# Two of the four weight sums of each seven-product pair: from VectorE additions to a plain transfer and an adding one

## The reference, cut to what matters

```python
hn = rmsnorm(h, norm_mlp_g[l])
x = h + jnp.square(jax.nn.relu(hn @ w_up[l])) @ w_down[l]        # 1024 -> 4096 -> 1024
...
h2 = rms_norm(x, ln2_g[l])
x = x + (jax.nn.silu(h2 @ w_ffn_gate[l]) * (h2 @ w_ffn_up[l])) @ w_ffn_down[l]   # 1024 -> 2816 -> 1024
```

## Time and profile before

| | |
|---|---|
| median of three runs | 1889.53 us |
| the profiled execution, its own time | 1890.52 us |
| span of its trace (first to last instruction) | 1888.7 us |
| TensorE busy | 1878.7 us (99%), granted clock 0.999 |
| VectorE busy | 1244.8 us (66%) |
| ScalarE busy | 775.0 us (41%) |
| GpSimd busy | 1088.0 us (58%) |
| DMA | 176.78 MB, 94 GB/s in the mean |

### The profile page before, as it was taken

The page is one execution under the profiler, slowest core; times in us unless marked ns, Lnnn a source line. Parts: engine busy times, 40 slices in busy tenths (PEclk is TensorE's granted clock), DMA queues, the critical chain, the costliest instruction groups (busy, mean ns, idle before and its releaser), DMA issues.

```text
span 1888.7 us, 31897 instructions
## 1 busy us (share of the span) xinstructions
PE 1878.7 (99%) x11737; PEld 1604.7 (85%) x11737; DVE 1244.8 (66%) x2116; ACT 775.0 (41%) x1523; POOL 1088.0 (58%) x1223
## 2 busy tenths in 40 slices
PE   9999999999999999999999999999999999999998
PEld 7788888888888888899989888888888888999997
DVE  7876777767642247767775468787721367888882
ACT  5344433444342245333433544655432344333333
POOL 5454345443445477767776844444555585666665
PEclk9999999999999999999999999999999999999999
DMA  4312220222223332332334322122233223323232
GB/s 160 98 48 89 78 77 28 83 89 67 68 81 109 133 97 93 101 101 92 110 101 128 135 100 79 56 67 79 79 134 104 96 90 100 112 91 112 93 109 78
DMA packets 53470, 176.78 MB, mean 94 GB/s; under 512 B 7744, under 2 KB 8576, under 8 KB 53120
## 3 DMA queue, kind: packets, MB, share of 16 engines
q1 hardware_dynamic: 52880, 172.85, 27.9%
q10 hardware_dynamic: 496, 2.65, 0.4%
HBM read 171.26 MB, written 4.23 MB: 93 GB/s over the span
## 4 chain that ended last, share of the span: by engine, by line
PE 98%; DVE 1%; POOL 0%; DMA 0%; ACT 0%; issue 0%; DVEq 0%
PE bank L322 18%; PE bank L324 17%; PE bank L323 17%; PE bank L860 5%; PE bank L862 5%; PE bank L861 5%; PE bank L910 5%; PE bank L911 5%; PE bank L912 5%; PE bank L2066 2%; PE bank L2060 2%; PE bank L2077 1%; PE bank L2317 1%; PE bank L2304 1%; PE bank L1277 1%; PE bank L1294 1%
## 5 line engine op out<-in xcount | busy, mean ns | idle before, releaser
L311 POOL TENSOR_TENSOR slab_lo<-slab_raw,slab_hi 128x256 fp32r<-128x256 f32 x1140 | 994.8, 907 | 750.0 <-ACT slab_hi L304 749.9
L322 PE MATMUL bank<-u_hi,slab_hi 128*128 128x512 f32 x1048 | 443.4, 423 | 0.2
L324 PE MATMUL bank<-u_hi,slab_lo 128*128 128x512 f32 x1048 | 410.9, 392 | 0.0
L323 PE MATMUL bank<-u_lo,slab_hi 128*128 128x512 f32 x1048 | 409.2, 390 | 0.0
L304 ACT CAST slab_hi<-slab_raw 128x1024 fp32r<-128x1024 f32 (+1 forms) x302 | 298.7, 999 | 88.5 <-PE bank L324 49.2
L324 PEld LDWEIGHTS bank<-u_hi,slab_lo 128*128 128x128 f32 x1048 | 196.7, 188 | 43.3
L322 PEld LDWEIGHTS bank<-u_hi,slab_hi 128*128 128x128 f32 x1048 | 197.3, 188 | 39.7 <-issue 4.1
L323 PEld LDWEIGHTS bank<-u_lo,slab_hi 128*128 128x128 f32 x1048 | 197.8, 189 | 34.2 <-issue 1.9
L910 PE MATMUL bank<-part_hi,slab_hi 128*128 128x512 f32 x384 | 150.0, 391 | 0.6 <-DVE residual L1824 0.6
L911 PE MATMUL bank<-part_lo,slab_hi 128*128 128x512 f32 x384 | 149.7, 390 | 0.0
L912 PE MATMUL bank<-part_hi,slab_lo 128*128 128x512 f32 x384 | 149.5, 389 | 0.0
(11 more groups left out here) (444 smaller groups left out, 3990.2 us busy)
## 6 DMA issues: line engine op xcount, KB each, us to landing
slab_raw<-slabs SPq DMA_DIRECT2D x302, 512.0 KB, 3.5
g_and_cum_rows<-row_store SPq DMA_DIRECT2D x7, 512.0 KB, 6.4
residual<-x_t SPq DMA_DIRECT2D x4, 512.0 KB, 7.0
residual<-x_t SPq DMA_DIRECT2D x1, 2048.0 KB, 9.3
residual_store<-residual SPq DMA_DIRECT2D x1, 2048.0 KB, 8.9
residual<-residual_store ACTq DMA_DIRECT2D x1, 2048.0 KB, 9.5
out_t<-result_tok SPq DMA_DIRECT2D x4, 256.0 KB, 2.4
out_t<-residual SPq DMA_DIRECT2D x4, 256.0 KB, 2.6
```

Of the source, the lines that this page charges most:

```text
L311: ins = pool.tensor_tensor(w_lo[s][:, ks, :], raw[s][:, ks, :], w_hi[s][:, ks, :].bitcast(F32), ALU.subtract)
L322: pe.matmul(bank, w_hi[s][:, k, :], x_hi[:, k, :], start=first, stop=False)
L323: pe.matmul(bank, w_hi[s][:, k, :], x_lo[:, k, :], start=False, stop=False)
L324: mm = pe.matmul(bank, w_lo[s][:, k, :], x_hi[:, k, :], start=False, stop=last)
```

## The change

For every seven-product pair, u1 and u3 are no longer added by VectorE. SP issues two plain transfers of 256 KB each from the weights in HBM into `w_sums_raw` (b.k1 into u1, a.k1 into u3); GpSimd waits for their landing and issues two accumulating transfers (b.k2 onto u1, b.k1 onto u3), which count up a semaphore `u_added`. VectorE waits for `u_added` and makes u2 and u4 as before. SP waits, before its two transfers, for both low halves of the pair before (`fast_u_lo`), and issues them ahead of the load of the slab that follows the pair. GpSimd issues its two ahead of the splits of the down slabs for the next gate (or of the pair in front, in the first block), and ahead of the splits of the up slabs for an up pair. Two semaphores are reused under new names.

```diff
@@ load_slab @@
+            if j % 2 == 0 and (ph, j // 2 - 1) in fast_of:
+                w_sums_begin(sp, ph, j - 2, fast_of[ph, j // 2 - 1])
             wait_slab(sp, s_lo, ph, i, j)
             if (ph, j // 2 - 2) in fast_of:
-                wait_again(sp, "fast_sum", 4 * fast_of[ph, j // 2 - 2] + 4)
+                wait_again(sp, "fast_sum", 2 * fast_of[ph, j // 2 - 2] + 2)
@@ the sums @@
-        def w_sums_first(dve, ph, j, f):
-            sa, sb = ph.slot(j), ph.slot(j + 1)
-            if f > 0:
-                wait_again(dve, "fast_u_lo", 2 * f)
-            dve.wait_ge(s_raw[sb], ph.landed(0, j + 1))
-            dve.tensor_tensor(ws_raw[:, f_u1], raw[sb][:, k1, :], raw[sb][:, k2, :], ALU.add)\
-                .then_inc(again("fast_sum"), 1)
-            dve.wait_ge(s_raw[sa], ph.landed(0, j))
-            dve.tensor_tensor(ws_raw[:, f_u3], raw[sa][:, k1, :], raw[sb][:, k1, :], ALU.add)\
-                .then_inc(again("fast_sum"), 1)
+        def w_sums_begin(sp, ph, j, f):
+            if f > 0:
+                wait_again(sp, "fast_u_lo", 2 * f)
+            wait_again(sp, "x_sum", 4 * QT * (1 if ph is ph_mlp else 2))
+            sp.dma_start(w_form(f_u1), w_part(ph, j + 1, k1)).then_inc(again("u_begun"), 16)
+            sp.dma_start(w_form(f_u3), w_part(ph, j, k1)).then_inc(again("u_begun"), 16)
+
+        def w_sums_first(pool, ph, j, f):
+            wait_again(pool, "u_begun", 32 * f + 32)
+            pool.dma_start(w_form(f_u1), w_part(ph, j + 1, k2), accum_op=ALU.add).then_inc(sem("u_added"), 16)
+            pool.dma_start(w_form(f_u3), w_part(ph, j + 1, k1), accum_op=ALU.add).then_inc(sem("u_added"), 16)
+
+        def w_sums_ahead(pool, ph, j):
+            g = j // 2
+            if j % 2 == 0 and (ph, g) in fast_of and ph is ph_ffn and FFN_GROUPS[g][0] == "up":
+                w_sums_first(pool, ph, j, fast_of[ph, g])
+            if j % 2 == 0 and (ph, g + 1) in fast_of and not (ph is ph_ffn and FFN_GROUPS[g + 1][0] == "up"):
+                w_sums_first(pool, ph, j + 2, fast_of[ph, g + 1])
 
         def w_sums_second(dve, ph, j, f):
             sa = ph.slot(j)
-            wait_again(dve, "fast_sum", 4 * f + 1)
+            dve.wait_ge(sem("u_added"), 32 * f + 32)
+            dve.wait_ge(s_raw[sa], ph.landed(0, j))
             dve.tensor_tensor(ws_raw[:, f_u2], ws_raw[:, f_u1], raw[sa][:, k1, :], ALU.add)\
                 .then_inc(again("fast_sum"), 1)
@@ mlp_pool, and the same in ffn_pool @@
+                w_sums_ahead(pool, ph_mlp, j + LEAD)
                 split_lo(pool, ph_mlp, 0, j + LEAD, fast_slab_start(ph_mlp, j + LEAD))
@@ mlp_dve; in ffn_dve three such calls @@
-                    if after:
-                        w_sums_first(dve, ph_mlp, 2 * MLP_FAST[f + 1], f + 1)
```

More of the change, by code:

```diff
@@ L250, in program @@
                  "fast_u_hi": "edif", "fast_u_lo": "v_rhs", "x_raw": "osum", "x_sum": "k_rhs", "x_hi": "eg",
-                 "x_lo": "cols", "down_half": "qk_ps"}
+                 "x_lo": "cols", "down_half": "qk_ps", "u_begun": "blk_ps", "tok_ps": "rsc"}
         LATER = {old: new for new, old in AGAIN.items()}
@@ L538, in turn @@
                     mm = pe.transpose(tok_banks[t][:, c * P:(c + 1) * P], h_res[:, m, t * P:(t + 1) * P], ident[:])
-                mm.then_inc(sem("tok_ps"), 1)
+                mm.then_inc(again("tok_ps"), 1)
         def norm_pe(pe, n):
@@ L761, in out_dve @@
             norm_dve(dve, n)
-            if n == 1:
-                w_sums_first(dve, ph_mlp, 2 * MLP_FAST[0], 0)
             if n in X_NORMS:
@@ L814, in x_sums_lo, with w_part @@
                 .then_inc(again("x_lo"), 1)
-        def w_sums_first(dve, ph, j, f):
-            sa, sb = ph.slot(j), ph.slot(j + 1)
-            if f > 0:
-                wait_again(dve, "fast_u_lo", 2 * f)
-            dve.wait_ge(s_raw[sb], ph.landed(0, j + 1))
-            dve.tensor_tensor(ws_raw[:, f_u1], raw[sb][:, k1, :], raw[sb][:, k2, :], ALU.add)\
-                .then_inc(again("fast_sum"), 1)
-            dve.wait_ge(s_raw[sa], ph.landed(0, j))
-            dve.tensor_tensor(ws_raw[:, f_u3], raw[sa][:, k1, :], raw[sb][:, k1, :], ALU.add)\
-                .then_inc(again("fast_sum"), 1)
+        def w_part(ph, j, ks):
+            src = dram["slabs"][bass.ds(ph.index(0, j), 1), :, ks.start * P:ks.stop * P]
+            return src.rearrange("a p n -> (a p) n")
@@ new lines, in w_form @@
+        def w_form(u):
+            return ws_raw[:, u].rearrange("p k c -> p (k c)")
+        def w_sums_begin(sp, ph, j, f):
+            if f > 0:
+                wait_again(sp, "fast_u_lo", 2 * f)
[6 more added lines that the diff above has]
+            pool.dma_start(w_form(f_u3), w_part(ph, j + 1, k1), accum_op=ALU.add).then_inc(sem("u_added"), 16)
@@ L831, in w_sums_second @@
             dve.tensor_tensor(ws_raw[:, f_u2], ws_raw[:, f_u1], raw[sa][:, k1, :], ALU.add)\
                 .then_inc(again("fast_sum"), 1)
-            wait_again(dve, "fast_sum", 4 * f + 3)
+            wait_again(dve, "fast_sum", 2 * f + 1)
             dve.tensor_tensor(ws_raw[:, f_u4], ws_raw[:, f_u2], raw[sa][:, k2, :], ALU.add)\
@@ L837, in w_sums_hi @@
         def w_sums_hi(act, f, h):
-            wait_again(act, "fast_sum", 4 * f + 3 + h)
+            wait_again(act, "fast_sum", 2 * f + 1 + h)
             if f > 0:
@@ L1787, in ffn_act @@
             for t in range(NT):
-                act.wait_ge(sem("tok_ps"), t + 1)
+                wait_again(act, "tok_ps", t + 1)
                 act.activation(tok_out[:, t, :], tok_banks[t][:], ACT.Copy, scale=r_col[:, t:t + 1])\
@@ L1843, in ffn_dve @@
                             silu(q, 1)
-                    elif before:
-                        w_sums_first(dve, ph_ffn, j + 2, before)
                     wait_again(dve, "fast_prod", 5 * f + 2)
@@ L1864, in ffn_dve @@
                     elif before:
-                        w_sums_first(dve, ph_ffn, j + 4, before)
                         w_sums_second(dve, ph_ffn, j + 4, before)
@@ L1885, in ffn_dve @@
                         f = fast_of[ph_ffn, g + 1]
-                        w_sums_first(dve, ph_ffn, j + 2, f)
                         w_sums_second(dve, ph_ffn, j + 2, f)
@@ L1939, in ffn_pool @@
                 if j + LEAD < ph_ffn.n:
+                    w_sums_ahead(pool, ph_ffn, j + LEAD)
                     split_lo(pool, ph_ffn, 0, j + LEAD, fast_slab_start(ph_ffn, j + LEAD))
```

## The result

The changed kernel takes 2010.2 us (median of 4 runs, 2007.7 to 2013.9) where the kernel before takes 1889.9 beside it: ratio 1.0637, 95% interval 1.0624 to 1.065. The profiled execution took 2009.6 us with a span of 2007.8. The forecast was 1938. So the direction was right, and 120 us stand where 48 were forecast: inside the range of 1898 to 2025, but in its part over 1975, which had a chance of 0.25.

The account below looks back on a forecast made before the run. TensorE, busy 1878.7 of 1888.7 us, was taken to bound the kernel. Late sums cost 46.5 us in the second block and 1.4 in the first, 48 onto 1890.5, so 1938 was forecast, range 1898 to 2025.

Parts of the forecast that it names:

- T: From the end of the low halves to the landing of GpSimd's adding transfers: 8.7 us, ends 6.4 and 14.1.
- x: Part of T: from SP's issue of its two plain transfers to their landing, 3.2 us.
- I: Part of T: GpSimd's issue of its two adding transfers, 2.0 us, ends 0.8 and 3.9.
- L: Part of T: landing of GpSimd's adding transfers, taken as twice the size, 3.5 us, ends 2.4 and 7.0.
- the formula: Second block: TensorE's added waits per period, 2T - 11.13 = 6.3 us, seven times, plus 2.4 for the first fast gate.
- VectorE's deadline holds: First block: GpSimd's transfers go at +1.1 and are added at +6.6, against 6.98, so VectorE's u2 is in time.
- the rival with slow transfers: Both blocks: T = 14.1 costs 127 us in the second and 33 in the first, together 2050; 0.25 for over 1975.
- The round of GpSimd: First block: landing, issues and splits take GpSimd 21.15 us against a period of 21.04; price 1.4 us over 13 pairs.
- since its clock and its matmuls stay: Whole kernel: at most 10.0 us could be had back from TensorE's waits, its clock and matmuls being unchanged.
- s1: Second block: TensorE's wait for the first residual addition in a down group, 2.0 us per period at T = 8.7.
- T - 6.69: Second block: the expression for s1, set by when the next gate's u1 and u3 arrive; 2.0 us at T = 8.7.

Follow-up runs that it names:

- not_adding: The changed kernel with GpSimd's two transfers overwriting instead of adding, so u1 and u3 lack a term: 1975.4 us in one run.
- two_buffers: The changed kernel with two alternating places each for u1 and u3 and SP's transfers begun one pair earlier, except each block's first pair: 1908.8 us, ratio 1.0096.
- splits_first: The changed kernel with GpSimd's two adding transfers issued behind the split of the slab they stood ahead of: 2081.7 us, ratio 1.101.
- kept_busy_ahead_of_product_6: The changed kernel with useless matmuls in the second block, 12 ahead of each gate's product 6, 4 and 10 in down groups: 1992.8 us, ratio 1.0546.
- sums_left_out: The kernel before with u1 and u3 left out for 30 of 32 pairs and no transfers in their place: 1888.05 us, ratio 0.9989.

## Why the prediction was right in kind and wrong in size

Profiled executions against each other, 71 us are missing in the forecast of 1938.5 (2009.6). They come from three terms.

1. *T, some 37 us.* The step "T = 3.2 + 2.0 + 3.5 = 8.7 us" was mis-sized; it measures 4.67 + 1.15 + 5.3 = 11.1. x: the second of SP's transfers is issued 0.4 behind the low half, takes 3.9 to land in the mean of the 16 chains, and GpSimd goes 0.3 later; the 2.8 of the earlier trace rows came from another stretch. I: the issues cost GpSimd 0.58 each until the next instruction can start, near SP's 0.40, not its 1.93. L: I took a transfer of half a megabyte for one that adds; the adding one needs 1.9 more than that, and `not_adding` shows 2.1 us for the adding alone. With the measured T the formula gives 22.26 - 11.13 = 11.1 us per period and 5.4 for the first gate, 83 us instead of 46.5.
2. *The first block, 21.9 us (23.3 less 1.4).* The step "VectorE's deadline holds" failed. GpSimd's transfers went at +2.9 and not +1.1 behind the pair, needed 1.15 + 5.4 instead of 2.0 + 3.5, and so were added at +9.5, not +6.6, against a deadline of 6.98. The +1.1 contradicts the prediction itself: the 5.3 us to the landing that it used for GpSimd's round, counted from 844.02, lead to +2.5, and its own 2.0 + 3.5 then to +8.0, already too late. The step had 0.4 us in hand on these numbers and got no end of the range; the rival with slow transfers had it, at 13 x 2.5 = 33 us. Of the 2.5 us per pair VectorE makes up 0.95 (7.61 from u2 to the end of the first addition, 8.56 before), which leaves 1.5; the pairs lost 1.2 each. The first pair's 7.5 us and the 1.5 ahead of it were in no term. The round of GpSimd, which I thought to be the price here, is 22.2 us instead of 21.15, but it follows TensorE: `two_buffers` has no such wait, `not_adding` with its faster landing alone keeps one such wait of 4.0, and `splits_first` is slower with GpSimd idle.
3. *The clock, some 12.5 us.* The account of what bounds the kernel says of TensorE "since its clock and its matmuls stay"; that new waits bring the clock down was no term at all. 95.8 us in the second block less the 83.3 of the formula is 12.5. The trace has a row for it: the 13.7 us by which products 6 and 7, which lie behind the wait for f_w, grew over eight gates, and `kept_busy_ahead_of_product_6` takes 11.4 of them away. The other steps that the sum took over from before moved as well, by up to 0.7 us per period, and nearly cancel: from u2 of the gate to the second low half 12.1 instead of 11.45, from u2 to f_w 1.8 instead of 2.39, from the start of U to its low half 2.6 instead of 2.99. The 39.2 us of longer busy time are more than the clock's price, which I read as follows: a slow matmul in D or ahead of a wait only takes from the next wait. No run shows that by itself. With the up pairs' wait alone, products 6 and 7 grow by 18.6 us.

What held: both places of the waits in the second block, their number and about their size (eight for f_w of 4.0 in the mean, eight for the first residual addition of 2.7), GpSimd's wait for a transfer ahead of its two issues, and the sentence that GpSimd's split takes its part of s1: in the period shown 1.22 + 2.86 = 4.1 us, against T - 6.69 = 3.7 with the 10.42 of that chain. What did not hold: TensorE in the first block was to stay within 5 us and lost 23.3, and VectorE's idle time ahead of L847 (128.8 us) is not its longest, which is 133.3 ahead of another line, as before (133.2). It is the longest that the change made. `sums_left_out` shows that VectorE's freed time is worth 2.0 us, not quite nothing. The two waits of a period nearly add: 53.5 + 47.2 alone, 94.2 together. Of the rivals, the one with slow transfers (2050 for T = 14.1) had the late sums of the first block, and the result stands nearer to it than to the forecast.

The best of the versions, with two places and early issues, ties with the kernel before; none that computes the right sums beats it.

## What to carry to other kernels

Work moved from a busy engine to transfers is priced by when the result is there, not by what the transfers cost: count the chain from the last reader of the buffer to the landing, and give it a second buffer and an early place in each issuing queue before anything else. A step whose slack is under the error of the terms in front of it is a term with a range, not a "holds". And a wait that a change adds to TensorE can have a second price behind it, here 1.7 us of slower matmuls per gate in the mean, behind waits of 4.0 in the mean; the gate with the shortest of them, 2.4, paid 0.1.

## What the runs showed of the hardware that I had not expected

- An adding transfer of 256 KB from GpSimd lands in 5.4 us, a plain one from the same queue in 3.3 (`not_adding`), SP's in 3.7, all at the median. In other versions the adding ones took 4.8 to 6.9.
- GpSimd's two issues together keep it from its next split for 1.15 us when the transfers add and for 1.11 when they don't. The first is 0.88 us long with the addition and 0.57 without.
- Behind a wait of 4.04 us TensorE's next 24 matmuls had 0.51 of the clock, and 194 useless matmuls ahead of such waits made a kernel 17.4 us faster, 11.4 us of which are products 6 and 7 at the higher clock again.
- An addition of VectorE with both inputs in SBUF takes 0.69 us alone. Started in the midst of a run of GpSimd's splits it took 3.1 to 3.6 us in the eight up pairs of `not_adding`.
- Twice 256 KB per pair by SP and twice by GpSimd beside two slabs of 512 KB cost nothing that can be measured when nobody waits for them (ratio 1.0006, 0.9997 to 1.0015).
